# Two blocks of a small network on one core: gathering each expert pass's features from token rows, one pass ahead

## The reference, cut to what matters

```
def expert_choice_ffn(h, w_router, w1, w3, w2):      # h: 256 tokens x 1024
    cap = (EC_CAPACITY_FACTOR * T) // N_EXPERTS        # 2 * 256 / 16 = 32
    aff = jax.nn.softmax((h @ w_router), axis=-1)
    gate, idx = lax.top_k(jnp.swapaxes(aff, 1, 2), cap)
    xe = h[bidx, idx]                                  # the gather
    hid = jax.nn.silu(einsum(xe, w1)) * einsum(xe, w3)
    ye = einsum(hid, w2) * gate[..., None]
    return jnp.zeros_like(h).at[bidx, idx].add(ye)
```

## Time and profile before

| | us |
|---|---|
| median of 3 runs | 3020.7 (3018.3 to 3021.01) |
| the profiled execution, its own time | 3020.67 |
| its span, first to last instruction | 3018.6 |
| TensorE busy in the span | 2675.2 (89%) |
| VectorE, ScalarE busy | 628.0 (21%), 446.7 (15%) |
| read from HBM | 695.30 MB |

### The profile page before, as it was taken

The page is one execution under the profiler, slowest core; times in us unless marked ns, Lnnn a source line. Parts: engine busy times, 40 slices in busy tenths (PEclk is TensorE's granted clock), DMA queues, the critical chain, the costliest instruction groups (busy, mean ns, idle before and its releaser), DMA issues.

```text
span 3018.6 us, 30042 instructions
## 1 busy us (share of the span) xinstructions
PE 2675.2 (89%) x12505; PEld 1833.6 (61%) x12505; DVE 628.0 (21%) x1331; ACT 446.7 (15%) x767; POOL 44.0 (1%) x55
## 2 busy tenths in 40 slices
PE   8999999999999999999989989888889997656656
PEld 7887778888888868888766553333224764111112
DVE  2011320113101321013133651121113242000002
ACT  1001310013002311003223420000002141000001
POOL 0000000000000001000000100000000000000000
PEclk9999999999999989999999999999999998777777
DMA  8445574457445569444421227999998205999996
GB/s 295 153 139 182 166 252 154 153 195 237 153 152 182 168 202 208 152 150 138 145 85 63 71 79 321 422 422 422 422 422 279 98 15 208 422 421 421 422 422 274
DMA packets 277022, 700.86 MB, mean 232 GB/s; under 512 B 16768, under 2 KB 198952, under 8 KB 229352
## 3 DMA queue, kind: packets, MB, share of 16 engines
q1 hardware_dynamic: 270432, 687.52, 61.9%
q10 hardware_dynamic: 4384, 7.54, 0.8%
q0 software_dynamic: 2112, 4.46, 0.7%
HBM read 695.30 MB, written 4.06 MB: 232 GB/s over the span
## 4 chain that ended last, share of the span: by engine, by line
PE 39%; DMA 20%; DVE 3%; issue 1%; ACT 1%; SPq 1%; DVEq 0%; ACTq 0%
PE bank L512 37%; DMA ring<-moe_w 20%; PE bank L521 2%; SPq L2709 1%; ACT AR L2169 1%; DVE AR L1419 0%; DVE AR L1422 0%; DVE AR L1431 0%; DVE H L1425 0%; ACT L2169 0%; DVE AR L1425 0%; DVE AR L1789 0%; DVE XC L1425 0%; DVE AR L2028 0%; DVE AR L2029 0%
## 5 line engine op out<-in xcount | busy, mean ns | idle before, releaser
L512 PE MATMUL bank<-H,ring 128*128 128x256 f32 (+1 forms) x5120 | 1148.2, 385 | 22.0 <-DVE H L1425 11.1
L512 PEld LDWEIGHTS bank<-H,ring 128*128 128x128 f32 (+1 forms) x5120 | 968.7, 190 | 191.0 <-issue 42.0
L512 PE MATMUL bank<-ring,AR 128*64 128x512 f32 (+2 forms) x2984 | 588.4, 716 | 228.9 <-DMA ring<-moe_w 224.4
L512 PEld LDWEIGHTS bank<-ring,AR 128*64 128x64 f32 (+2 forms) x2984 | 180.1, 142 | 631.2 <-issue 559.4
L512 PE MATMUL bank<-AR,ring 128*128 128x256 f32 (+2 forms) x1504 | 333.5, 380 | 5.1 <-DVE AR L1431 5.1
L512 PE MATMUL bank<-AR 128*128 128x512 f32 (+13 forms) x1048 | 317.3, 472 | 17.7 <-ACT AR L2169 5.3
L512 PEld LDWEIGHTS bank<-AR,ring 128*128 128x128 f32 (+2 forms) x1504 | 283.8, 189 | 47.9 <-DVE AR L1431 5.6
L2169 ACT ACTIVATE AR<-bank 128x512 f32<-128x512 f32 (+4 forms) x196 | 116.2, 594 | 1269.6 <-PE bank L512 921.9
L1419 DVE TENSOR_TENSOR AR<-bank,AR 128x512 f32<-128x512 f32 (+2 forms) x105 | 72.3, 689 | 837.3 <-PE bank L512 790.6
L512 PEld LDWEIGHTS bank<-AR 128*128 128x128 f32 (+7 forms) x1048 | 161.3, 188 | 129.4 <-issue 99.4
L1419 DVE TENSOR_TENSOR AR<-AR,bank 128x512 f32<-128x512 f32 (+1 forms) x112 | 70.0, 630 | 757.0 <-PE bank L512 756.9
(11 more groups left out here) (106 smaller groups left out, 614.6 us busy)
## 6 DMA issues: line engine op xcount, KB each, us to landing
ring<-moe_w SPq DMA_DIRECT2D x371, 1024.0 KB, 16.1
ring<-ffn_w SPq DMA_DIRECT2D x132, 1024.0 KB, 5.4
ring<-ada_w SPq DMA_DIRECT2D x48, 1024.0 KB, 5.3
ring<-m_w_in SPq DMA_DIRECT2D x26, 1024.0 KB, 5.4
ring<-even_w_in SPq DMA_DIRECT2D x24, 1024.0 KB, 5.1
ring<-m_w_out SPq DMA_DIRECT2D x8, 1024.0 KB, 9.6
ring<-ple_gate SPq DMA_DIRECT2D x8, 1024.0 KB, 4.9
ring<-even_w_out SPq DMA_DIRECT2D x8, 1024.0 KB, 5.0
```

The costliest lines, as they stand in the source:

```text
L512: ins = pe.matmul(o, lhsT, rhs, start=start, stop=stop, skip_group_check=True)
```

## The change

1. `XE` and the gathers that fill it are gone. A pass's features are made in the pass in front: TensorE multiplies the token rows `TM` (stationary, 128 x 128) by only this pass's columns of `PM` (64 columns for each of two streams in layer 0, 128 in layer 1), right into the two banks 4 and 5, and ACT and DVE copy them to `XCUR`. That is 32 matmuls per pass in layer 0 and 16 in layer 1. Since an operand's address can't follow the loop, DVE's `pick` first copies the pass's columns to `PMC`.
2. The first pass's features are gathered ahead of the loop (`gather_first`): the context stream's part of layer 0 now after `affinity_turns`, the other after `one_hots`. DVE copies the index columns (L2082) after the first features instead of in front.
3. The loop is turned: an iteration is now gather of pass i+1, `y` of pass i, `h1` and `h3` of pass i+1, `scatter` in one piece, `turn_hidden`; the last `y` stands behind the loop. DVE does `accumulate`, `one_hot` and only then the copy of the transposed half; `MACC` is cleared ahead of the first such copy.
4. `MACC`, `P1` and `P3` move into the room of `XE`, so `TM` and `PM` stay whole.
5. `EARLY` has 6 and 9 chunks, at other places and with earlier waits: 18 and 21 MB lie ready. In layer 0 the first waits for the end of the attention (`x.o11`, `ye_x`), in layer 1 for `mla.o7`, `yo_ready` or the scaled features.

```diff
-        XE = area(0, KT, 2 * NE * CAP)
-        XE1 = area(0, KT, NE * CAP)
-        MACC = [area(8192, KT, 2 * S), area(8192, KT, S)]
+        MACC = [area(0, KT, 2 * S), area(0, KT, S)]
+        P1, P3 = [area(4096, D), area(10240, D)], [area(5120, D), area(11264, D)]
+        PMC = area(14152, S)
...
-        EARLY = [{7: "products", 12: "tokens_c", 13: "h0", 14: "h1", 15: "tokens"},
-                 {12: "products", 13: "values", 14: "queries", 15: "gates", 16: "xc", 17: "h0", 18: "h1", 19: "tokens"}]
+        EARLY = [{5: 4096, 11: 6144, 12: 0, 13: 2048, 14: "h0", 15: "h1"},
+                 {7: 6144, 8: "hot_c", 9: 10240, 10: "xc", 15: 0, 16: 2048, 17: 4096, 19: "h0", 20: "h1"}]
...
+                def gather(name, l, streams, hot, i=None):
+                    ns, slots, groups, _ = experts(l)
+                    for half in range(2):
+                        b = tiles[f"{name}{half}"][0]
+                        for j in range(4):
+                            o = bank[b][:, j * P:(j + 1) * P].rearrange("p (g s c) -> p g s c", s=ns, c=CAP)
+                            for s in streams:
+                                for t in range(2):
+                                    mm(o[:, :, s, :], TM[:, 2 * s + t, paired(4 * half + j)], hot(2 * s + t),
+                                       j == 0 and s == ns - 1 and t == 0, t == 1,
+                                       full[b] if j == 3 and s == 0 and t == 1 else None)
...
                     if l == 0:
-                        gather(0, 1, 0, 3, (4, 5, 6, 7))
                         late_sum("moe0", 0)
-                        gather(0, 1, 3, KT, (4, 5, 6, 7))
...
                     affinity_turns(l, 0, 3)
+                    if l == 0:
+                        gather_first(0, 1)
                     index_rows(l, 0, 0)
-                    gather(l, 0, 0, KT, range(8))
-                    slot_rows(l, 0)
+                    gather_first(l, 0)
+                    slot_rows(l, 6)
...
+                    up(f"m{l}.p.", None)
+                    turn_hidden(f"m{l}.p.", None)
                     with pe.Fori(0, passes - 1) as i:
                         loads.loop(i, groups)
-                        one_pass(f"m{l}.", i)
+                        for half in range(2):
+                            fill(f"m{l}.x{half}", 4 + half, i, STEP[4 + half])
+                        pe.wait_ge(sig("picked"), before - l + 1 + i)
+                        gather(f"m{l}.x", l, range(ns - 1, -1, -1),
+                               lambda n: PMC.rearrange("p (t g c) -> p t g c", g=groups, c=CAP)[:, n], i)
+                        by_weights(f"m{l}.y", 6, HIDT, i)
+                        up(f"m{l}.", i)
+                        scatter(i)
+                        turn_hidden(f"m{l}.", i)
+                    by_weights(f"m{l}.z.y", 6, HIDT, None)
...
+                    def pick(n):
+                        w = groups * CAP
+                        dve.tensor_copy(PMC.rearrange("p (t n) -> p t n", n=w),
+                                        PM[:, 0:2 * ns, bass.ds(n * w, w)]).then_inc(sig("picked"), 1)
...
-                    gather(0)
                     gated_hidden(f"m{l}.p.", None)
-                    turned_hidden(f"m{l}.p.", None)
                     step(dve.memset(MACC[l], 0.0))
                     one_hot(0)
+                    turned_hidden(f"m{l}.p.", None)
                     with dve.Fori(0, passes - 1) as i:
-                        gather(i + 1)
+                        pick(i + 1)
+                        b = filled(dve, f"m{l}.x1", i)
+                        dve.tensor_copy(XCUR[:, 4 * P:8 * P], bank[b][:, :]).then_inc(free[b], 1)
                         gated_hidden(f"m{l}.", i)
-                        accumulate(f"m{l}.", i, before + 1 + i, 0, 4)
+                        accumulate(i)
+                        one_hot(i + 1)
                         turned_hidden(f"m{l}.", i)
-                        accumulate(f"m{l}.", i, before + 1 + i, 4, KT)
-                        one_hot(i + 1)
```

More of the change, by code:

```diff
@@ L1260, in gather @@
                             emptied(pe, f"tm{l}.{2 * s + t}{g}")
[L1261 to L1265, removed]
+                    if s == ns - 1:
+                        for half in range(2):
+                            fill(f"m{l}.p.x{half}", 4 + half)
+                    gather(f"m{l}.p.x", l, (s,), lambda n: PM[:, n, 0:groups * CAP].rearrange("p (g c) -> p g c", c=CAP))
                 def slot_rows(l, b):
@@ L1333, in turn_hidden @@
                                 f = 4 * half + j
[L1334 to L1342, removed]
+                                turn(bank[b][:, j * P:(j + 1) * P], P3[l][:, paired(f)], full[b] if j == 3 else None)
@@ L1343, in scatter, with up @@
+                    def scatter(i):
+                        emptied(pe, f"m{l}.ya", i)
+                        emptied(pe, f"m{l}.yb", i)
+                        pe.wait_ge(pg_ready, before + 1 + i)
+                        for k in range(KT):
+                            b = fill(f"m{l}.f{k}", k % 4, i, STEP[k % 4])
                             mm(bank[b][:, 0:nt], YS[:, k * P:(k + 1) * P], PG[:, 0:nt], True, True, full[b])
-                    def one_pass(pre, i):
-                        pe.wait_ge(xcur_ready, before + 1 if i is None else before + 2 + i)
+                    def up(pre, i):
+                        emptied(pe, f"{pre}x0", i)
+                        emptied(pe, f"{pre}x1", i)
@@ L2076, in moe @@
                     one_hots(l, 0)
-                    for k in range(1, KT, 2):
-                        gathered(l, 0, k)
+                    take(f"m{l}.p.x1", XCUR[:, 4 * P:8 * P], lambda b: b[:, :])
                     b = filled(dve, f"ic{l}")
@@ L2624, in moe, with gate, turned, rows @@
                     token_rows(l, 0, 1)
-                    for k in range(0, KT, 2):
-                        gathered(l, 0, k)
-                    def one_pass(pre, i):
+                    take(f"m{l}.p.x0", XCUR[:, 0:4 * P], view=lambda b: b[:, :])
+                    def gate(pre, i):
                         for half in range(2):
                             b = filled(act, f"{pre}h1{'ab'[half]}", i)
-                            f(P1[:, half * 512:(half + 1) * 512], bank[b][:, :], ACT.Silu).then_inc(free[b], 1)
+                            f(P1[l][:, half * 512:(half + 1) * 512], bank[b][:, :], ACT.Silu).then_inc(free[b], 1)
+                    def turned(pre, i):
                         b = filled(act, f"{pre}t0", i)
                         f(HIDT[:, 0:512], bank[b][:, :], ACT.Copy).then_inc(free[b], 1)
+                    def rows(pre, i):
                         for half in range(2):
```

85 lines of the change are left out of this document (30 added, 55 removed).

## The result

The changed kernel takes 3030.87 us (median of 9, 3024.21 to 3033.39) against 3020.57 us of the kernel before (median of 9, 3018.3 to 3022.93). The ratio is 1.0031, with a 95% interval of 1.0022 to 1.0040. Forecast were 3012.0 us, faster.

A forecast was written before the change was run, and what follows sets the result against it. The prediction took weight transfers to pace the expert passes. From 3020.67 us, layer 0 would lose 7 (two to three slow-clock passes) and layer 1 gain 15.5, giving 3012.2; 2997 to 3034 was to hold 8 in 10.

The forecast's parts named there:

- the rival by which TensorE becomes layer 0's bound: Layer 0's passes: from 3.7 fallen passes of 7 on the whole is slower, 3038 with all; chance 0.22.
- Layer 0: Expert passes of layer 0: end of the last `y` at 2293.2, 7 us later, with two to three slow-clock passes.
- The start of the first in-loop gather: Layer 0, ahead of the first `y`: 33.7 us after the first product at 1817.5.
- the head: Layer 0 ahead of its passes: norm sum, router and gather changes bring the first product 16.8 us earlier, at 1817.5.
- The first gather itself: Layer 0, ahead of the first `y`: 32 small matmuls take 12.4 us, since PE idled four us before.
- The pass with the clock kept: One layer 0 pass on TensorE at 2.4 GHz: 57.5 us, with a gather of 6.8 and 1.4 idle.
- The slack under the transfers: Layer 0's passes: TensorE's 57.5 us stays 2.2 us under the transfers' 59.66, at 2.4 GHz.
- The number of falls: Layer 0's passes whose gather drops PE's clock: two to three of seven, counted as 2.5 at 7.2 us each.
- none: Rival, layer 0: the clock holds, at most one pass falls; 6 us earlier to 2 later, say 3003; chance 0.33.
- The head's gain is given back: Layer 0: loads rest until the first `y` releases chunks and resume at 1870.1, 0.9 us later than before.
- Layer 1: Second expert layer: 15.5 us earlier, from gather 12.0, faster clock 1.0 and ninth early chunk 2.5.
- Isolated matmuls: Gather of 32 in layer 0's loop: the skill's formula would give 3.8 us; the prediction held to trace rows instead.

The follow-up runs named there:

- fill1: Changed kernel with one dense product of 512 columns, result unused, at the head of each of layer 0's iterations: 3012.28 us, ratio 0.9965.
- split: Changed kernel with layer 0's transposes between two halves of the scatter and the pick made one pass ahead: 3012.12 us, ratio 0.9964.
- split_clear: `split` with the clearing of `MACC` and the first one-hot moved behind the turned hidden rows and first pick, both layers: 3005.73 us, ratio 0.9945.
- halves: `split_clear` with `y` ahead of the gather as in `swap`, and waits for DVE's half of each copy only before the third chunk: 2991.34 us, ratio 0.9907.
- l1_only: Layer 0 as in the kernel before, layer 1 as in the changed kernel: 3005.05 us, ratio 0.9942.
- late_clear: Changed kernel with only the clearing of `MACC` and the first one-hot behind the turned hidden rows, first pick still last: 3034.99 us, ratio 1.0046.
- early5: `split_clear` with five instead of six early chunks in layer 0: 3007.68 us, ratio 0.9956.
- swap: Changed kernel with `y` of each pass ahead of the gather in TensorE's order, both layers: 3018.95 us, ratio 0.9991.

## Why the prediction was wrong

Right were most terms of the sum, and that the layers add up; wrong were the size of layer 0 and with it the sign. The case that came is the rival by which TensorE becomes layer 0's bound, from 3.7 fallen passes on. It had 0.22.

**Layer 0: + 28.3 us where + 7 was forecast.** By the terms of the sum:

- *The start of the first in-loop gather*: 1858.09, forecast 1817.5 + 33.7 = 1851.2, 6.9 late. Of these 2.2 had arisen ahead of the change (the attention's last matmuls began at 1778.72 and 1776.54). 2.7 are the head, which gained 1834.35 - 1822.36 + 2.2 = 14.2 where some 16.8 were forecast: 4.1 for 5.0 as far as the router's end, as the norm sum took 2.07 us in place of 1.03 and the router 5.38 in place of 3.63, both at 0.50 behind a gap; 1.1 in the first gather, 7.1 for 6.0; 0.7 behind it, where the index product took 1.03 in place of 0.61 and a faster one had been counted as a gain. Some 2.0 lie between first product and gather: w1 and w3 took 29.2 for 27.8, since the clock rose only within their first 33 product records (9.04 us), and the wait behind them was 6.5 for 5.9.
- *The first gather itself*: 13.91 for 12.4, 1.5 more; PE was at 0.50 from its start, after 4.91 of idling.
- *The pass with the clock kept*: 58.4 for 57.5. The small matmul costs 0.24 and not 0.21 (7.7 for 6.8); the gap was 1.09, not 1.4; the rest of the pass took some 49.6, not 49.3. Over seven passes, the last without a gather, 5.9. The slack under the transfers was 1.2 us and not 2.2.
- *The number of falls*: I took 2.5 at 7.2 each, 18. It was four at 64.5 - 58.4 = 6.1, 24.3: 6.3 more. The size of a fall was right within 1.1 us, their number was not.
- Waits for weights in two passes: 0.7.

6.9 + 1.5 + 5.9 + 6.3 + 0.7 = 21.3; measured against the forecast of 2293.2 are 2314.35 - 2293.2 = 21.2.

Three terms failed: the count of falls, 2.5 where four came; the slack, 2.2 us a pass where it was 1.2; and the start of the first `y`, 8.4 us later than forecast (the first two terms above). For the count I had no row that said how often a gap of a little over 1 us next to small matmuls drops the clock, only one that said it can, and spread the chances evenly over "none", "two to three" and "nearly all". The slack stood on the lower of two prices (0.21 worked out from weight loads, where the nearest matmuls had shown 0.23) and on passes of 49.3. The count alone doesn't explain the sign: with 2.5 falls of 6.1 layer 0 would still have lost 19.1 us, about the 18.6 that layer 1 and the end give back (an estimate from the terms above). `fill1` and `split` show that the gap decides, and that without falls behind the first gather the transfers set the pace again. They come out near the forecast's 3012, but with no later fall where it had 2.5, so they don't bear it out.

**The head's gain is given back**: right, and more than that. Loads rested until 1878.99, 9.8 us later than before, where 1870.1 and 0.9 were forecast; 8.4 of the difference are the first two terms above. `split_clear` to `halves` show the converse: what the first `y` gains comes out at the end. It starts at 1866.11, 1860.44 and 1850.80, and layer 0 ends at 2289.59, 2282.10 and 2273.86: 5.7 and 9.6 us at the one place, 7.5 (with 1.7 of slow beginning saved) and 8.2 at the other. Of the 1.4 missing in the second pair the trace shows the likely cause: in `halves` the loads resume ahead of the first gather, which frees no slot of the ring, and the transfers dip once more (82 GB/s from 1877 to 1878). I had seen that the clearing of `MACC` and the gather stand ahead of that `y`, but not that both can simply be moved.

**Layer 1: 17.3 us earlier where 15.5 were forecast.** From the gather's start to the first product 18.67 became 6.58, 12.1 (12.0). From there to the resuming of the loads 6.14 became 4.61, 1.5 (1.0). The ninth early chunk gave 2.45 (2.5). Another 1.2 came back between the layers, and 1.3 in the very last products, whose clock I had not looked at. `l1_only` measures the whole at 17.8.

**Isolated matmuls.** The Trainium skill ("TensorE: Matmul & The Clock Gate", section Back-to-back issue gap) has a formula for an isolated matmul, from which the prediction's estimate of 3.8 us for a gather came. In all kernels a gather took 7.75 at the upper clock level. The section's own warning, that the formula under-counts at small N since it has no budget for the weight load, agrees with the trace: PEld was busy throughout.

## What to carry to other kernels

A step of few columns per weight load, put into a loop of dense matmuls, has two prices: its own time, bound by the weight loads, and the clock's, if there is idling of a microsecond on either side of it (here 0.98 to 1.09 us). Look for work that can stand on both sides of it without a wait (in `halves` half of a copy was enough to start), before counting on the slack under the transfers: here 1.2 us in 60 was used up by the first fall. And where a stage's stream rests until a first release, it is the start of that release that sets the end: move whatever stands ahead of it.

## What the runs showed of the hardware

- In `swap` a gap of 1.27 us between transposes and dense products left the granted clock at 1.00. Gaps of 0.98 to 1.09 us beside 7.7 us of 128x64 matmuls mostly took it to 0.50: ahead of them in 4 of 6 cases (changed kernel), 5 of 6 (`late_clear`) and in `split_clear` and `early5`, behind them in 7 of 7 (`swap`), there in front of dense products. Without a gap the small matmuls kept 1.00, in all six later gathers of `split` and all seven of `halves`.
- What picks the falls among equal gaps of 1.09 us was not settled; no run here varies it alone. In the kernel before, too, a gap of 1.82 us ahead of layer 0's first products left the clock at 1.00 (1834 to 1860), and one of 1.84 ahead of layer 1's was followed by 0.50.
- Behind a fall the clock came back only under dense products, with 1.7 to 2.5 us lost after the gather's end: in the changed kernel 192 product records took 43.3 to 44.1 us in place of 41.6.
- The price of a float32 matmul with a full stationary operand and 64 columns is 0.24 us at the upper level and 0.43 at the lower.
